# The first two dense panels cut into quarters and laid between the first modulation sums

## The reference

```
mod = silu(c) @ w_mod[0] + b_mod[0]           # (2048) x (2048 x 6144)
shift, scale, gate = split(mod, 3)
h = x * (1 + scale) + shift                   # 256 x 2048
q, k, v, g = split(h @ a_w_in, 4)             # (256 x 2048) x (2048 x 8192)
```

## Time and profile before

| | us |
|---|---|
| median of three runs | 2608.76 |
| the profiled execution | 2612.34 |
| its span (first to last instruction) | 2610.6 |
| TensorE busy in it | 2410.5 (92%) |
| VectorE busy | 1792.1 (69%) |
| ScalarE busy | 1051.9 (40%) |

### The profile page before, as it was taken

One profiled execution on the slowest core, in us unless ns is written; L12 is line 12 of the kernel. 1 busy time (PEld: TensorE's weight loads), 2 busy tenths in 40 slices (PEclk: granted clock), 3 DMA queues, 4 the chain that ended last, 5 costly groups with the idle time before them and its releaser, 6 DMA issues.

```text
span 2610.6 us, 42057 instructions
## 1 busy us (share of the span) xinstructions
PE 2410.5 (92%) x17599; PEld 2008.8 (77%) x17599; DVE 1792.1 (69%) x2871; ACT 1051.9 (40%) x1588; POOL 186.1 (7%) x290
## 2 busy tenths in 40 slices
PE   5799999999889899989999696999799999999998
PEld 1488887777656698788887494788798998998986
DVE  4548887988767666977887657677654677555545
ACT  0243334454542323343663322444444443443443
POOL 1103433010100000112000000000000000000000
PEclk7799999999899899989999758999899999999999
DMA  9969999798877689979778898788355678655553
GB/s 353 337 223 349 372 360 319 240 349 300 319 278 276 226 301 339 386 262 317 241 255 320 244 346 298 238 275 270 125 186 191 227 268 281 211 192 185 187 169 106
DMA packets 317516, 699.72 MB, mean 268 GB/s; under 512 B 13648, under 2 KB 14160, under 8 KB 312464
## 3 DMA queue, kind: packets, MB, share of 16 engines
q1 hardware_dynamic: 298496, 627.29, 69.5%
q0 software_dynamic: 18560, 67.66, 7.3%
q10 hardware_dynamic: 272, 2.10, 0.2%
HBM read 646.78 MB, written 56.49 MB: 269 GB/s over the span
## 4 chain that ended last, share of the span: by engine, by line
PE 70%; DVE 16%; DMA 10%; ACT 2%; issue 1%; SPq 1%; DVEq 0%; ACTq 0%
PE bank L2281 68%; DVE ring_lo L1424 4%; DVE arena L1424 3%; DMA ring<-in_w_mod 3%; DVE sm L1424 2%; DMA ring<-in_a_w_in 2%; PE bank L2284 2%; DVE LT L1432 2%; DMA ring<-in_kv_w 2%; DVE arena L1432 2%; DMA ring<-in_b_w_out 1%; DVE MSB L1424 1%; DMA ring<-in_b_w_in 1%; DMA ring<-in_kv_w_mod 1%; DMA arena<-arena 1%
## 5 line engine op out<-in xcount | busy, mean ns | idle before, releaser
L1424 DVE TENSOR_TENSOR ring_lo<-ring,w_hi 128x1024 fp32r<-128x1024 f32 (+1 forms) x380 | 428.3, 1135 | 355.9 <-ACT w_hi L1022 335.1
L1022 ACT CAST w_hi<-ring 128x1024 fp32r<-128x1024 f32 x316 | 330.2, 1048 | 473.5 <-PE bank L2281 473.4
L1022 ACT CAST att_w_hi<-ring 128x1024 fp32r<-128x1024 f32 x192 | 197.1, 1048 | 327.3 <-DMA ring<-in_kv_w 118.8
L1424 DVE TENSOR_TENSOR ring_lo<-ring,att_w_hi 128x1024 fp32r<-128x1024 f32 x192 | 233.7, 1221 | 125.7 <-ACT att_w_hi L1022 124.8
L2281 PE MATMUL bank<-in_hi,w_hi 128*128 128x256 f32 x1024 | 290.3, 283 | 1.1 <-ACT n L969 1.1
L2281 PE MATMUL bank<-in_lo,w_hi 128*128 128x256 f32 x1024 | 290.2, 283 | 0.0
L2281 PE MATMUL bank<-in_hi,ring_lo 128*128 128x256 f32 x1024 | 289.8, 283 | 0.0
L2281 PE MATMUL bank<-w_hi,hid_lo 128*128 128x512 f32 x640 | 254.2, 397 | 0.4 <-DVE ring_lo L1424 0.4
L2281 PE MATMUL bank<-att_w_hi,att_hi 128*128 128x512 f32 x512 | 209.7, 410 | 12.2 <-DVE ring_lo L1424 12.2
L2281 PE MATMUL bank<-ring_lo,att_hi 128*128 128x512 f32 x512 | 203.9, 398 | 0.0
L2281 PE MATMUL bank<-att_w_hi,att_lo 128*128 128x512 f32 x512 | 203.5, 397 | 0.0
(11 more groups left out here) (276 smaller groups left out, 5087.7 us busy)
## 6 DMA issues: line engine op xcount, KB each, us to landing
ring<-in_w_mod SPq DMA_DIRECT2D x192, 1024.0 KB, 9.3
ring<-in_a_w_in SPq DMA_DIRECT2D x64, 1024.0 KB, 9.4
ring<-in_w_mlp_in SPq DMA_DIRECT2D x64, 1024.0 KB, 5.2
ring<-in_w_mlp_out SPq DMA_DIRECT2D x64, 1024.0 KB, 5.1
ring<-in_kv_w_mod SPq DMA_DIRECT2D x32, 1024.0 KB, 9.9
ring<-in_kv_w SPq DMA_DIRECT2D x32, 1024.0 KB, 8.2
ring<-in_b_w_in SPq DMA_DIRECT2D x32, 1024.0 KB, 5.9
ring<-in_s_w_glu SPq DMA_DIRECT2D x32, 1024.0 KB, 5.2
```

The costliest lines, as they stand in the source:

```text
L1022: a.copy(whi(h), raw_half(h)).then_inc(*o.up("whi"))
L1424: return v.tensor_tensor(dst, x, y, op).then_inc(*(to or o.up("dve")))
```

## The change

`mod(0)` now holds the first 512 columns of the shift and `mod(1)` those of the scale, so that with every second modulation one quarter of x can be finished. x is turned first of all and copied out of PSUM by ScalarE. After `mod(0)` and `mod(1)` come four rounds r = 1 to 4: `mod(2r)`, four tiles of panel 0 (k = 4(r-1) to 4r-1), the sums of `mod(2r)`, `mod(2r+1)`, the same four tiles of panel 1, its sums. In rounds 2 and 3 four `state` pieces follow each four tiles. So `mod(8)` and `mod(9)` come in round 4 and no longer behind panels 0 and 1. Tiles 0 to 31 are renumbered in this order (`tile_of`): 0 to 3 panel 0, 4 to 7 panel 1, 8 to 11 panel 0, and so on. `x_quarter(q)` on both engines makes quarter q of the input: VectorE adds bias, scales two of four column blocks and splits off lo, ScalarE scales the other two and makes hi. `discretise` is cut up between the quarters and the tiles. `s5_b` and `s5_c` are loaded from the last load of `mod(1)` on. From panel 2 on the order is as before (`TILES_B` is 34 for 36).

```diff
-MODS = ([("m0s", nt) for nt in range(0, 32, 4)] + [("m2a", nt) for nt in range(0, 32, 4)]
+MODS = ([("m0s", nt + half) for nt in range(0, 16, 4) for half in (0, 16)] + [("m2a", nt) for nt in range(0, 32, 4)]
...
-MOD_AT_PRE = {pn: 8 + pn for pn in range(8)}
+MOD_AT_PRE = {pn: 8 + pn for pn in range(2, 8)}
...
-TILES_FIRST, TILES_B, TILES_CL, TILE_M2A = 24, 36, 156, 152
+TILES_B, TILES_CL, TILE_M2A = 34, 156, 152
...
+ROUNDS = range(1, 5)
+def tile_of(i):
+    if i >= 32:
+        return divmod(i, 16)
+    return i % 8 // 4, 4 * (i // 8) + i % 4
...
+def round_order(r):
+    a, b = 2 * r, 2 * r + 1
+    return (a, 0), (a, 1), (a, 2), (a, 3), "first", (b, 0), (b, 1), (b, 2), (b, 3), "second"
+STATES_AT = {(2, "first"): 0, (2, "second"): 4, (3, "first"): 8, (3, "second"): 12}
...
@@ GpSimd @@
-            g.wait_ge(*landed("mod", 7, 3))
+            g.wait_ge(*landed("mod", 1, 3))
@@ ScalarE @@
-            for j in range(8):
-                mod(j)
+            for k2 in range(8):
+                a.wait_ge(*filled("xt", 0, k2))
+                copy(x_raw[:, 2 * k2:2 * k2 + 2, :], bank("xt", 0, k2)[:, :].rearrange("p (j n) -> p j n", j=2), *empty("xt", 0, k2))
+            mod(0)
+            mod(1)
...
-            split_in(0, x_raw, sc1, M("m0", 0), 1, PHk)
+            def x_quarter(q):
+                a.wait_ge(S["scol"], q + 1)
+                if q == 0:
+                    own()
+                for k in (4 * q + 2, 4 * q + 3):
+                    act(x_raw[:, k, :], x_raw[:, k, :], ACT.Identity, scale=sc1[:, k:k + 1], bias=M("m0", k, 1))
+                a.wait_ge(S["xmod"], q + 1)
+                own()
+                in_hi(PHk, x_raw, q)
+            x_quarter(0)
...
+            for r in ROUNDS:
+                for part, j in (("first", 2 * r), ("second", 2 * r + 1)):
+                    i0 = 8 * (r - 1) + 4 * (part == "second")
+                    mod(j)
+                    for i in range(i0, i0 + 4):
+                        tile(i)
+                    if (r, part) in STATES_AT:
+                        s0 = STATES_AT[r, part]
+                        for s in range(s0, s0 + 4):
+                            state(s)
+                if r < 4:
+                    x_quarter(r)
@@ VectorE @@
-            for _ in discretise():
-                pass
-            mod_bias("m0s")
-            own()
-            ts(sc1, M("m0", 16), 1.0, None, ADD, None, *o.up("scol"))
-            split_in(0, x_raw, sc1, M("m0", 0), PHk, PLk, "pre")
...
+            def x_quarter(q):
+                at, ks = MOD_OFF["m0"] + 4 * q, (4 * q, 4 * q + 1)
+                v.wait_ge(S["mod_sum"], 2 * q + 2)
+                tt(MODC[:, at:at + 4], MB0[:, at:at + 4], C("bm", 4 * q, 4), ADD)
+                tt(MODC[:, at + 16:at + 20], MB0[:, at + 16:at + 20], C("bm", 16 + 4 * q, 4), ADD, *o.up("mod_bias"))
+                own()
+                ts(sc1[:, 4 * q:4 * q + 4], M("m0", 16 + 4 * q, 4), 1.0, None, ADD, None, *o.up("scol"))
+                v.wait_ge(*emptied("xt", 0, 2 * q))
+                own()
+                for k in ks:
+                    ts(x_raw[:, k, :], x_raw[:, k, :], sc1[:, k:k + 1], M("m0", k, 1), MUL, ADD,
+                       *o.up("xmod" if k == ks[1] else "dve"))
+                in_lo(PLk, PHk, x_raw, q, "pre")
+            discretised(10)
+            x_quarter(0)
+            tiles(4)
+            discretised(5)
+            tiles(8)
+            x_quarter(1)
+            discretised(1)
+            tiles(12)
+            discretised(2)
+            tiles(16)
+            x_quarter(2)
+            discretised(2)
+            tiles(20)
+            discretised(2)
+            tiles(24)
+            x_quarter(3)
+            discretised(4)
+            tiles(26)
             v.wait_ge(*emptied("st", "b", 7))
             own()
             tt(tmpb, bT[:, 1], bcw(tci), MUL)
-            tiles(TILES_FIRST + 2)
             v.wait_ge(*filled("st", "c", 7))
             tt(Bb[:, 0], bT[:, 0], bcw(tcr), MUL)
-            tiles(TILES_FIRST + 4)
             own()
             tt(Bb[:, 0], Bb[:, 0], tmpb, SUB)
-            tiles(TILES_FIRST + 6)
+            tiles(28)
...
@@ TensorE @@
+            p.wait_ge(S["x"], 16)
+            turn_in(0, x0)
             p.wait_ge(S["cact"], 2)
...
+            mod(0)
+            mod(1)
+            sums(1)
...
+            for r in ROUNDS:
+                for what in round_order(r):
+                    if what in ("first", "second"):
+                        i0 = 8 * (r - 1) + 4 * (what == "second")
+                        for i in range(i0, i0 + 4):
+                            pre_tile(i)
+                        j = 2 * r + (what == "second")
+                        if j < 9:
+                            sums(j)
+                        if (r, what) in STATES_AT:
+                            s0 = STATES_AT[r, what]
+                            for i in range(s0, s0 + 4):
+                                state(i)
+                        continue
+                    j, q = what
+                    mod_part(j, q)
+                if r == 1:
+                    p.wait_ge(S["lam_cols"], 1)
...
```

More of the change, by code:

```diff
@@ L185, in tile @@
     def tile(i):
-        pn, k = divmod(i, 16)
+        pn, k = tile_of(i)
         if k == 0:
@@ L194, in tables @@
         bank.use(("cols", i), GA)
-    for j in range(8):
-        mod(j)
-        if j == 4:
-            bank.use(("lam",), GA)
     for k in range(8):
         bank.use(("xt", 0, k), GV)
-    for i in range(16 * N_PRE):
+    mod(0)
[3 more added lines that the diff above has]
+            if what in ("first", "second"):
+                i = 8 * (r - 1) + 4 * (what == "second")
+                for j in range(4):
+                    tile(i + j)
+                if (r, what) in STATES_AT:
+                    s0 = STATES_AT[r, what]
+                    for s in range(s0, s0 + 4):
+                        bank.use(("st", "bc"[s // 8], s % 8), GC)
+                continue
+            j, q = what
+            ring.use(("mod", j, q), slots)
+            if q == 0:
+                bank.use(("mod", j), GM)
+        if r == 1:
+            bank.use(("lam",), GC)
+    for i in range(32, 16 * N_PRE):
         pn, k = divmod(i, 16)
         tile(i)
-        if pn == 1 and k < 8:
-            for s in (2 * k, 2 * k + 1):
-                bank.use(("st", "bc"[s // 8], s % 8), GC)
         for ch in range(16):
@@ L721, in sync_program @@
                 sp.dma_start(dst, src).then_inc(S["rows"], 16)
-            for j in range(8):
-                mod(j)
-            for pn in range(N_PRE):
+            mod(0)
+            mod(1)
+            for r in ROUNDS:
+                for what in round_order(r):
+                    if what in ("first", "second"):
+                        pn = int(what == "second")
+                        load(("proj", pn), win, 0, 512 * pn, r - 1)
+                    else:
+                        j, q = what
+                        load(("mod", j), MOD_W[MODS[j][0]], 0, 128 * MODS[j][1], q)
+            for pn in range(2, N_PRE):
                 load_w(("proj", pn), win, 0, 512 * pn)
@@ L1809, in bcw, with discretised @@
                 return x.unsqueeze(2).to_broadcast([128, 128, 16])
-            tiles(TILES_FIRST)
+            making = discretise()
+            def discretised(n):
+                for _ in range(n):
+                    next(making, None)
+            def x_quarter(q):
[29 more added lines that the diff above has]
+            tiles(26)
             v.wait_ge(*emptied("st", "b", 7))
@@ L2578, in unit_factors @@
                 t.then_inc(*fill("fu"))
-            for pn in range(N_PRE):
+            for r in ROUNDS:
+                for what in round_order(r):
+                    if what in ("first", "second"):
+                        i0 = 8 * (r - 1) + 4 * (what == "second")
[4 more added lines that the diff above has]
+                            sums(j)
+                        if (r, what) in STATES_AT:
+                            s0 = STATES_AT[r, what]
+                            for i in range(s0, s0 + 4):
+                                state(i)
+                        continue
+                    j, q = what
+                    mod_part(j, q)
+                if r == 1:
+                    p.wait_ge(S["lam_cols"], 1)
+                    room("lam")
+                    for i, s_ in enumerate((cr, ci, lbr, lbi)):
+                        t = tr(bank("lam")[:, 128 * i:128 * i + 128], s_)
+                    t.then_inc(*fill("lam"))
+            for pn in range(2, N_PRE):
                 for k in range(16):
                     pre_tile(16 * pn + k)
-                    if pn == 1 and k < 8:
-                        state(2 * k)
-                        state(2 * k + 1)
                     for ch in range(16):
```

55 lines of the change are left out of this document (32 added, 23 removed).

## The result

The kernel after takes 2618.8 us (median of 12 executions, 2609.9 to 2624.1), the kernel before, timed beside it, 2608.5. The ratio is 1.0042, with a 95% interval from 1.003 to 1.0054: some 11 us slower. (One of the twelve executions of the kernel before took 4151.9 us; the other eleven lie between 2601.7 and 2611.5.) The forecast was 2621, with 2615 to 2632 as its own range.

The account below looks back on a forecast made before the run. TensorE bounds the stage from tile 32, so its start decides: 99.6 + 73.1 + 23.5 = 196.2 at full clock, about 208.3 with clock losses, against 196.1 before. 2608.8 + 12 = 2621 us, range 2615 to 2632.

Parts of the forecast that it names:

- tile 0: First tile of panel 0: its load lands at 69 and it starts at 70.6 us, against 115.8 in the kernel before.
- tile 8, without the slow clock of tiles 4 to 7: After `sums(3)` end at 90.8, 8.8 us of ScalarE and VectorE work put tile 8's start at 99.6.
- work from tile 8 to 32: TensorE's own work: 24 tiles 34.3, 16 states 15.8, `mod(5)` to `mod(9)` 18.2, five sums 4.8; 73.1 us.
- waits before tiles 12, 20, 28: ScalarE copies the modulation ahead of the casts, so TensorE waits 2.05 us each, 6.2 together.
- wait before tile 16: A 14.5 us chain through ScalarE and VectorE, two `tau` pieces included; TensorE covers 7.6, leaving a wait of 6.9.
- wait before tile 24: The same chain as before tile 16, with `tau` 7 and the last copies: a wait of 5.1 us.
- before tile 26: slow clock of tiles 24, 25 and the wait: Three Bbar operations in a row on VectorE, 8.2 us against two tiles' 2.9: a wait of 5.3.
- clock, the other tiles from 4 to 31: Half pace after idles: 8.8 us at tiles 4, 8, 16 and 26, plus 3.3 for three 2 us idles.
- even halves: Unused alternative: the queues share DMA equally beside `s5`, giving the ring 130 GB/s and tile 0 1.6 us earlier.
- Unchanged distance to the end: From tile 32 on TensorE is the bound and its order untouched, so the stage takes the same time as before.
- TensorE would fill the DMA time: Rival: half of the 28.6 us of waits hide, clock holds, tile 32 at 183, time 2596; chance 0.22.
- A clock that stays full: Rival: waits as forecast but full clock after idles of 2 to 7 us; tile 32 at 196.2, 2609; chance 0.17.

Follow-up runs that it names:

- filler: The changed kernel plus 6 to 36 identity transposes on TensorE before tiles 0, 4, 8, 12, 16, 20, 24, 26 and 28: 2611.2 us, ratio 1.0013.
- all three: The changed kernel with `tau` pieces moved, casts ahead of the modulation copy, and Bbar operations spread, together: 2595.3 us, ratio 0.9958 to the kernel before.
- Bbar edit: The changed kernel with VectorE's six Bbar operations spread out instead of three in a row before tile 26: 2614.3 us, ratio 1.0028.
- pieces moved: The changed kernel with VectorE's `tau` pieces moved, four after tile 11 and four after tile 19: 2609.0 us, ratio 1.0003 to the kernel before.
- casts first: The changed kernel with ScalarE's copy of the modulation's bank behind the four tiles' casts, not ahead: 2610.5 us, ratio 1.0014 to the kernel before.
- eight states: The changed kernel with all eight states of a round behind its first four tiles, none behind the second four: 2615.5 us, ratio 1.003.
- `s5` later: The changed kernel with the 16 `s5` loads started at the last load of `mod(3)` instead of `mod(1)`: 2615.4 us, ratio 1.0028.
- no piece before 8: All three plus eight states, with the bank `lam` copy and its piece moved from before tile 8 to behind tile 11: 2597.5 us, ratio 0.9968.
- all and filler: All three plus identity transposes on TensorE, 18 before tile 0 and 20 before tile 8: 2603.4 us, ratio 0.9991 to the kernel before.
- all three again: The same kernel as all three, timed once more on one chip beside all and filler: 2595.5 us, ratio 0.9966 to the kernel before.

## Why the prediction was right

**Step by step.** Expected and measured:

| step | expected | measured |
|---|---|---|
| tile 0 | 70.6 | 70.70 |
| tile 4 | 84.1 | 85.55 |
| tile 8, without the slow clock of tiles 4 to 7 | 99.6 | 100.9 (102.41 with it) |
| work from tile 8 to 32 | 73.1 | 75.0 |
| waits before tiles 12, 20, 28 | 2.05 each | 1.95 each |
| wait before tile 16 | 6.9 | 7.20 |
| wait before tile 24 | 5.1 | 5.26 |
| before tile 26: slow clock of tiles 24, 25 and the wait | 5.3 | 2.34 + 2.58 |
| clock, the other tiles from 4 to 31 | 12.1 | 10.0 |
| tile 32 | 208.3 | 209.2 |
| time | +12 | +11 |

That tile 32 is met to 0.9 us is partly luck: the start of tile 8 (+1.3) and the work behind it (+1.9, most of it in the states, 17.0 us for 15.8) were priced too low, the clock (-2.1) too high. The waits, on which the forecast rests, are right by themselves: 23.5 us expected and 23.2 measured, with the slow clock of tiles 24 and 25 counted in, as the forecast did.

- The transfers: `s5` starts at 36.80 (expected 35.4), and DMA moves 269 GB/s from 40 to 68 us, 259 in the earlier trace rows. By the sum of the forecast the ring got 119 GB/s of it (7.5 MB less 4.19), not 109, and the last load of `mod(1)` came 0.8 us later (36.27 for 35.47); the two cancel, and tile 0 is met to 0.1 us. The Trainium skill (DMA: Bandwidth & Descriptors, Queues, rings and completion order) has each DMA engine take turns between its queues by whole packets. The forecast's estimate made even halves of that, with tile 0 at 1.6 us earlier; the trace doesn't agree with even halves of the bytes (119 of 269).
- Tiles 4 and 8: I saw that the modulation's copy stands ahead of the casts before tiles 12, 20 and 28, but not that it also does before tile 4 (2.04). With the clock's 1.5 us in the tiles from 4, that is what tile 8 is late by.
- The 2 us waits and those before tiles 16 and 24: right in place, cause and size; moving the casts removed the first, moving the pieces took 5.2 and 3.2 from the others.
- Before tile 26: I set 8.2 us of VectorE against two tiles at full pace (2.9), and wrote that the slow clock of tile 24 hides in this wait. It does: tiles 24 and 25 ran at half pace and took 5.46 instead of 3.12, and 8.2 - 5.46 = 2.7 is left as a wait. Together 4.9, for 5.3. Only the sign to look for was wrong, a wait of some 5 us: a wait and a slow clock in front of it show as one or the other. When the pieces were moved and tile 24 ran at full clock, the wait was 4.93, and tile 26 started the same 8.04 us after tile 24.
- The clock: the eight groups from tile 4 on take 7.46, 8.03, 5.99, 8.17, 7.50, 5.46, 4.29 and 7.31 us, where full pace is 5.98 for four tiles, 3.12 for two, and 5.72 from the start of tile 28 to that of 32: 12.4 together, or 10.0 without tiles 24 and 25. Of the four short idles (1.95 or 2.04 us, tile 4's among them) one (tile 12) left the clock full, and three cost 1.5 to 1.6 each. I had let half of three fall at 2.2 and priced tile 4 as one of the long ones. The long idles before tiles 8 and 16 cost 2.05 and 2.2. The experiment with the filler got 8 us of the time back.
- "Unchanged distance to the end" held only roughly. Of 13.1 us at tile 32, about 11 arrive at the end by the medians. TensorE's waits on tile lo, first in the kernel before from 196 to 393 us, then in the kernel after over the same work:

```profile
PE bank L2281 <- DVE ring_lo L1424: 2.5, 8, 0.8
```

```profile
PE bank L2382 <- DVE ring_lo L1496: 0.3, 2, 0.2
```

VectorE and ScalarE were late there before, and a TensorE that comes later finds its tiles ready: 2.2 us given back. But the distance doesn't stay there. By ScalarE's copies of the modulations, in this pair of executions, it is 9.9 from 520 to 650 us, 12.3 at 870, 12.3 at 1468, and 6.9 at the next copy, where the kernel before waited 4.54 us for a load and the kernel after 1.01. The profiled executions end 6.8 apart, the medians 10.2. This last step belongs to the execution and not to the change: the kernel with all three, traced twice, has both. Its distance to the kernel before goes there from -14.7 to -15.4 in the first trace (a wait of 4.0 for a load) and from -12.8 to -18.4 in the second (1.6). Where the median's 2 to 3 us go stays open.

**The rivals.** That TensorE would fill the DMA time (2596) is not what the change does, but nearly what it could do: with three placements mended the time is 2595. What the forecast held against it is what the edits show: the waits follow from the order of each program, and when the order is mended they go. A clock that stays full would have given 2609; the two halves of the loss, waits and clock, are shown apart by the edits to the pieces and the casts (-10 and -7) and the filler (-8). These overlap, since each removed wait also spares a fall of the clock; together the three edits give -22 where their sum is -21 (the Bbar edit's 4 being within the noise). The 28.6 us of waits in the first rival don't come out of its terms: 196.2 less 168 is 28.2, which changes its 2596 by a fifth of a us.

**The measure.** How the sums move and how the time does, kernel less kernel before (time by the ratio):

| kernel | sums | time |
|---|---|---|
| after | +13.0 | +11.0 |
| pieces moved | +2.3 | +0.8 |
| casts first | +1.0 | +3.7 |
| Bbar spread | +12.7 | +7.3 |
| all three | -10.4 | -11.0 |
| eight states | +9.0 | +7.8 |
| `s5` later | +7.5 | +7.3 |
| no piece before 8 | -5.7 | -8.3 |
| filler | +6.4 | +3.4 |
| all and filler | -3.8 | -2.3 |
| all three again | -10.9 | -8.9 |

One moment read from one trace tells the time to within 3 us, but for the Bbar edit (5.4). Set against the change instead of the kernel before, three more are 3.5 to 4.6 us off (casts first, all and filler, all three again). That the rest only shifts holds to that measure.

## What to carry to other kernels

A reordering of loads is worth what the engines between the load and the bound let through: for each new piece, write down what stands ahead of its cast and its split in these engines' own programs, and put side work before the wait for the piece, not after it. A pause is where the engine would otherwise wait, and only as long as that; a piece placed right behind it lands on the path. A filler for the clock must not need anything that the idle's own cause holds back. And a wait for the last engine of a chain is followed up to the first before it is called that engine's: in the kernel with no piece before tile 8 it was a load.

## What had not been expected of the hardware

- An idle of 1.95 us may or may not cost the clock, and the fall can come behind it: after tile 12's the matmuls stay 0.12 us apart, after tile 20's they are 0.21 apart from the first, and after tile 28's 0.12 until 202.6, 0.21 until 205.9, then 0.12 again. The last in TensorE's timeline of the kernel after (columns as in the earlier trace rows):

```profile
202.31 0.28 PE L2382 MATMUL bank<-hid_lo,in_lo 128*128 128x256 f32 x1
203.32 0.41 PE L2382 MATMUL bank<-hid_lo,in_lo 128*128 128x256 f32 x1
206.20 0.28 PE L2382 MATMUL bank<-hid_lo,ring_lo 128*128 128x256 f32 x1
```

- In the kernel after the idles of 4.2 us and more were all followed by half pace from the first matmul. The Trainium skill (TensorE: Matmul & The Clock Gate, HAM oscillation — how this bites in real kernels) tells of waits of 3 to 5 us for a load; the rows here add that 2 us can be enough. The length of an idle alone doesn't decide it: with the filler 1.29 us before tile 4 was followed by half pace, and 2.10 us before tile 26 by full pace.
- `s5`'s loads cost the ring far more than their bytes: before they start it moves 384 GB/s (from 40 to 61 us, in the experiment in which they come later), with them DMA moves 266 to 269 in all. In 28 us the ring loses some 7.4 MB (of 10.8) for their 4.19. The forecast had this from the earlier trace rows; the experiment shows that it doesn't hang on the place.
